# Sample sequences in a gated-linear-attention head: output rows from masked queries in groups of 32 array columns, and state updates from values stacked as rounded part over remainder

## What is computed

```python
q_dec   = q * exp(bcum)              # bcum: running sum of the log decay
k_intra = k * exp(-bcum)
k_state = k * exp(blast - bcum)
att     = where(causal, q_dec @ k_intra.T, 0)
o_intra = att @ v
# per chunk:
o_inter = q_dec @ s                  # s: 128 x 512 state of the head
s       = exp(blast) * s + k_state.T @ v
```

## Time and profile before

| what | value |
|---|---|
| median of 3 runs | 1750.68 us (1748.29 to 1751.83) |
| time of the profiled execution | 1749.48 us |
| its span | 1747.8 us |
| mean granted PE clock | 0.978 |
| PE busy | 1669.8 us, 96% of the span |
| DVE, ACT, POOL busy | 810.9, 481.5, 395.2 us |
| chain that ended last, share on PE | 88% |

### The profile page before, as it was taken

One profiled execution on the slowest core, in us unless ns is written; L12 is line 12 of the kernel. 1 busy time (PEld: TensorE's weight loads), 2 busy tenths in 40 slices (PEclk: granted clock), 3 DMA queues, 4 the chain that ended last, 5 costly groups with the idle time before them and its releaser, 6 DMA issues.

```text
span 1747.8 us, 26517 instructions
## 1 busy us (share of the span) xinstructions
PE 1669.8 (96%) x10399; PEld 1581.4 (90%) x10399; DVE 810.9 (46%) x1188; ACT 481.5 (28%) x1017; POOL 395.2 (23%) x386
## 2 busy tenths in 40 slices
PE   6899999999999999987999999999999999999997
PEld 3799999999999999987998899988999889998796
DVE  4494449443944394456133551234612346213365
ACT  4321111111111111134343313443032531225323
POOL 3221121211221122114132112241212322113210
PEclk8999999999999999988999999999999999999998
DMA  9412212221222122111012111122111121111212
GB/s 351 131 53 73 75 39 65 74 76 39 65 74 76 39 65 74 51 37 37 26 42 79 64 41 49 31 67 79 39 49 37 61 79 39 48 37 55 79 43 102
DMA packets 145621, 115.23 MB, mean 66 GB/s; under 512 B 5885, under 2 KB 128345, under 8 KB 145506
## 3 DMA queue, kind: packets, MB, share of 16 engines
q1 hardware_dynamic: 143680, 112.87, 21.0%
q10 hardware_dynamic: 1834, 0.74, 0.2%
HBM read 99.05 MB, written 15.00 MB: 65 GB/s over the span
## 4 chain that ended last, share of the span: by engine, by line
PE 88%; DVE 8%; ACT 2%; issue 1%; DMA 1%; SPq 0%; ACTq 0%; DVEq 0%
PE psA L506 45%; PE psB L506 29%; PE psB L1798 2%; PE psB L1748 2%; PE psB L1765 2%; PE psX L1730 1%; DVE PQ L1257 1%; PE psX L1787 1%; PE psB L1756 1%; DMA ada<-in_ada_w 1%; DVE y_rows L1499 1%; PE psX L1612 1%; DVE a_hi L582 1%; ACT PQ L1035 1%; DVE PQ L422 0%
## 5 line engine op out<-in xcount | busy, mean ns | idle before, releaser
L313 POOL TENSOR_TENSOR w_lo<-stage,w_hi 128x1024 fp32r<-128x1024 f32 x112 | 279.0, 2491 | 1069.5 <-ACT w_hi L308 1069.5
L506 PE MATMUL psA<-h_hi,w_hi 128*128 128x362 f32 (+1 forms) x1152 | 279.9, 352 | 28.3 <-DVE h_lo L444 15.6
L506 PEld LDWEIGHTS psA<-h_hi,w_hi 128*128 128x128 f32 x1152 | 200.3, 193 | 77.7 <-issue 73.4
L506 PE MATMUL psA<-h_lo,w_hi 128*128 128x362 f32 (+1 forms) x1152 | 255.9, 331 | 0.0
L506 PE MATMUL psA<-h_hi,w_lo 128*128 128x362 f32 (+1 forms) x1152 | 255.7, 330 | 0.0
L308 ACT ACTIVATE w_hi<-stage 128x1024 fp32r<-128x1024 f32 x112 | 120.2, 1073 | 392.2 <-PE psB L506 301.3
L506 PEld LDWEIGHTS psA<-h_hi,w_lo 128*128 128x128 f32 x1152 | 203.1, 191 | 0.0
L506 PEld LDWEIGHTS psA<-h_lo,w_hi 128*128 128x128 f32 x1152 | 203.0, 191 | 0.0
L506 PE MATMUL psB<-h_hi,w_hi 128*128 128x362 f32 (+1 forms) x576 | 129.4, 333 | 1.7 <-ACT kT L1035 1.7
L506 PE MATMUL psB<-h_hi,w_lo 128*128 128x362 f32 (+1 forms) x576 | 126.7, 328 | 0.0
L506 PE MATMUL psB<-h_lo,w_hi 128*128 128x362 f32 (+1 forms) x576 | 126.7, 328 | 0.0
(11 more groups left out here) (297 smaller groups left out, 2307.4 us busy)
## 6 DMA issues: line engine op xcount, KB each, us to landing
stage<-in_gla_w_in SPq DMA_DIRECT2D x40, 512.0 KB, 3.8
stage<-in_pool_w_in SPq DMA_DIRECT2D x32, 512.0 KB, 4.1
ada_stage<-in_ada_w SPq DMA_DIRECT2D x24, 512.0 KB, 3.8
ada<-in_ada_w SPq DMA_DIRECT2D x8, 1024.0 KB, 12.5
stage<-in_pool_w_out SPq DMA_DIRECT2D x16, 512.0 KB, 3.4
v<-in_state_gla SPq DMA_DIRECT2D x32, 256.0 KB, 2.6
out_new_gla_sample<-v SPq DMA_DIRECT2D x32, 256.0 KB, 2.0
stage<-in_gla_w_out SPq DMA_DIRECT2D x16, 512.0 KB, 3.6
```

The lines of the kernel that those rows point to most:

```text
L313: nc.gpsimd.tensor_tensor(w_lo[:, j % 2, :], stage[:, j % 2, :], w_hi[:, j % 2, :].bitcast(f32), ALU.subtract).then_inc(lay.lo_done, 1)
L506: last = nc.tensor.matmul(ps[u][:, t, 0:width], weight(w[:, p, :], k), a[:, k, n0:n0 + width], start=(k == 0 and pas == 0), stop=(k == kt ...
```

## The change

It rearranges the samples' part of the GLA heads:

- Masks, `att_s`, `ksm` and `ksT_s` now have 128 partitions: the 64 sample rows stand twice, in the lower and the upper half. The values of the samples move from `v[0:64, 8, :]` to `v_s`, which holds their rounded part in rows 0 to 63 and the remainder in rows 64 to 127; `v_rows` on DVE makes both. `ksm` is made as rounded part and remainder (two DVE operations in a chain, one buffer of each).
- The state update of a sequence becomes two fp32r matmuls of 128 x 128 by 128 x 512 (`sample_update`).
- The queries are written into `qd_cols`, 8 of every 32 columns, the rest zero. `sample_inter` uses 32 such columns as weights and the old state, 512 wide, as moving operand; sequence b writes PSUM partitions 32(b mod 4) on. It runs for two sequences at a time in the even iterations 2, 4, 6 and 8. Sequences 4 to 7 add onto 0 to 3, in other rows of the same groups.
- After the last of them ACT copies the rows to SBUF (`smp_rows`), and `sample_out` on PE, in iteration 9, first does the intra part with the attention's rounded part and remainder (8 fp32r matmuls), then turns the rows to columns and sorts them with 4 f32 matmuls.
- Transposes of the samples' values, of their keys and their scores are written as two f32 matmuls each, into the lower and the upper 64 partitions.
- The samples' output and the mean squares move from bank `X[1]` to bank `X[0]`; `mean_square` gets a wait for the attention mask of the next chunk.
- POOL's setup has more operations; some small buffers move to memory that is reused later.

```diff
                 def ks_rows(b):
-                    if b >= 2:
-                        dve.wait_ge(smp_upd, g * NB + b - 1)
-                    nc.vector.tensor_scalar(ksm[:, b % 2, :], ksT_s[:], seq_rows[:, b:b + 1], None,
-                                            ALU.mult).then_inc(ksm_ready, 1)
+                    if b >= 1:
+                        dve.wait_ge(smp_upd, g * NB + b)
+                    link(nc.vector.tensor_scalar(ksm[:, 0, :], ksT_s[:], seq_rows[:, b:b + 1], None, ALU.mult))
+                    nc.vector.scalar_tensor_tensor(out=ksm[:, 1, :], in0=ksT_s[:], scalar=seq_rows[:, b:b + 1],
+                                                   in1=ksm[:, 0, :].bitcast(f32), op0=ALU.mult,
+                                                   op1=ALU.subtract).then_inc(ksm_ready, 1)
...
-                    nc.vector.tensor_copy(v[0:NS, NSUP, i * P:(i + 1) * P], ps[1][0:NS, 2, 0:P])\
+                    link(nc.vector.tensor_copy(v_s[:, i * P:(i + 1) * P], ps[1][:, 2, 0:P]))
+                    nc.vector.tensor_tensor(v_s[NS:P, i * P:(i + 1) * P], ps[1][NS:P, 2, 0:P],
+                                            v_s[NS:P, i * P:(i + 1) * P].bitcast(f32), ALU.subtract)\
                         .then_inc(L1.evac[1], 1)
...
-                nc.vector.copy_predicated(att_s[:], causal_s[:], X[0][0:NS, 0:NS]).then_inc(smp_attr, 1)
+                link(nc.vector.copy_predicated(att_s[:], causal_s[:], X[0][:, 0:NS]))
+                link(nc.vector.tensor_copy(att_hi[:], att_s[:]))
+                nc.vector.tensor_tensor(att_lo[:], att_s[:], att_hi[:].bitcast(f32),
+                                        ALU.subtract).then_inc(smp_attr, 1)
...
                 gate_in(2)
+                act.wait_ge(smp_rows_done, g + 1)
+                nc.scalar.activation(smp_rows, X[1], ACT.Copy).then_inc(smp_rows_out, 1)
                 split_slot(L1, GP, act, g, GP.slot["O01"])
                 o_out(NSUP)
...
-                def sample(b):
-                    pe.wait_ge(s0_loaded[b % 4], g * 32 + (b // 4) * 16 + 16)
-                    for e in range(KG):
-                        c = 256 + e * NS + b * TS
-                        last = nc.tensor.matmul(X[1][:, c:c + TS], v[:, b, e * P:(e + 1) * P],
-                                                qd_s[:, b * TS:(b + 1) * TS], start=False,
-                                                stop=(b == NB - 1 and e == KG - 1), skip_group_check=True)
+                def sample_inter(b0):
+                    for b in (b0, b0 + 1):
+                        pe.wait_ge(s0_loaded[b % 4], g * 32 + (b // 4) * 16 + 16)
+                        first = b < 4
+                        rows = slice(CG * (b % 4), CG * (b % 4) + CG)
+                        c = CG * b + (TS if first else 0)
+                        last = nc.tensor.matmul(X[1][rows, :], qd_cols[:, c:c + CG], v[:, b, :], start=first,
+                                                stop=not first)
                     if b == NB - 1:
-                        last.then_inc(smp_o_done, 1)
+                        last.then_inc(smp_rows_done, 1)
+                def sample_update(b):
...
-                    nc.tensor.matmul(ps[1][:, 2, :], ksm[:, b % 2, :], v[0:NS, NSUP, :], start=True,
+                    nc.tensor.matmul(ps[1][:, 2, :], ksm[:, 0, :], v_s[:], start=True, stop=False)
+                    nc.tensor.matmul(ps[1][:, 2, :], ksm[:, 1, :], v_s[:], start=False,
                                      stop=True).then_inc(smp_upd, 1)
+                def sample_out():
+                    pe.wait_ge(smp_attr, g + 1)
+                    for e in range(KG):
+                        for part in (att_hi, att_lo):
+                            nc.tensor.matmul(X[0][:, 256 + e * NS:256 + (e + 1) * NS], v_s[:, e * P:(e + 1) * P],
+                                             part[:], start=(e == 0 and part is att_hi), stop=False,
+                                             skip_group_check=True)
+                    pe.wait_ge(smp_rows_out, g + 1)
+                    for e in range(KG):
+                        last = nc.tensor.matmul(X[0][:, 256 + e * NS:256 + (e + 1) * NS], smp_rows[:, e * P:(e + 1) * P],
+                                                smp_order, start=False, stop=(e == KG - 1), skip_group_check=True)
+                    last.then_inc(smp_o_done, 1)
...
-                sample_intra()
                 fill(FILL_START - 5)
...
                     if 1 <= s <= NSUP:
+                        pe.wait_ge(att_ready, g * NSUP + min(s + 2, NSUP))
                         mean_square(s - 1)
+                    if s in (2, 4, 6, 8):
+                        sample_inter(s - 2)
+                    if s == NSUP + 1:
+                        sample_out()
                     if s >= 2:
-                        sample(s - 2)
+                        sample_update(s - 2)
```

More of the change, by code:

```diff
@@ L172, in trunk @@
         Kp = sb("Kp", [P, 4, SUP], stack=heads)
-        qd_s = sb("qd_s", [P, NS], stack=heads)
         ki_s = sb("ki_s", [P, NS], stack=heads)
         ks_s = sb("ks_s", [P, NS], stack=heads)
-        ksT_s = sb("ksT_s", [NS, P], stack=heads)
-        v = sb("v", [P, NSUP + 1, GW], stack=heads)
+        ksT_s = sb("ksT_s", [P, P], stack=heads)
+        att_lo = sb("att_lo", [P, NS], f32r, stack=heads)
+        v = sb("v", [P, NSUP, GW], stack=heads)
+        v_s = sb("v_s", [P, GW], f32r, stack=heads)
         heads.close()
@@ L185, in trunk @@
         a_lo = sb("a_lo", [P, KG, T], f32r)
+        qd_s = qd_cols[:, TS:TS + NB * CG].rearrange("p (b c) -> p b c", c=CG)[:, :, 0:TS]
+        smp_rows = Kp[:].rearrange("p b t -> p (b t)")
+        smp_order = ident[:].rearrange("p (j c) -> p j c", c=CG)[:, :, 0:2 * TS]\
+            .rearrange("p j (h t) -> p h j t", h=2)
         s1 = PQ[:, 0:WE]
@@ L276, in trunk @@
         S_stored = sem("S_stored")
+        smp_rows_done, smp_rows_out = sem("smp_rows_done"), sem("smp_rows_out")
         smp_o_done, smp_o_evac, smp_ksT = sem("smp_o_done"), sem("smp_o_evac"), sem("smp_ksT")
@@ L804, in _ @@
                                     pattern=[[1, P]], channel_multiplier=-1))
[L806 to L817, removed]
+            link(pool.memset(seq_two[:], 1.0))
@@ new lines, in _ @@
+            link(pool.affine_select(out=seq_two[:], in_=seq_two[:], compare_op=ALU.is_ge, fill=0.0, base=0,
+                                    pattern=[[-NS, 2], [-TS, NB]], channel_multiplier=1))
+            link(pool.affine_select(out=seq_two[:], in_=seq_two[:], compare_op=ALU.is_ge, fill=0.0, base=TS - 1,
+                                    pattern=[[NS, 2], [TS, NB]], channel_multiplier=-1))
+            link(pool.tensor_tensor(seq_rows[:], seq_two[:, 0, :], seq_two[:, 1, :], ALU.add))
@@ new lines, in _ @@
+            causal_two = mod1[:].rearrange("p m c -> p (m c)")[:, 0:2 * NS].rearrange("p (h c) -> p h c", h=2)
+            for h in range(2):
+                cs3 = causal_two[:, h, :].rearrange("p (b t) -> p b t", b=NB)
+                link(pool.memset(cs3, 1.0))
+                link(pool.affine_select(out=cs3, in_=cs3, compare_op=ALU.is_ge, fill=0.0, base=-NS * h,
+                                        pattern=[[-TS, NB], [0, TS]], channel_multiplier=1))
+                link(pool.affine_select(out=cs3, in_=cs3, compare_op=ALU.is_ge, fill=0.0, base=NS * h,
+                                        pattern=[[TS, NB], [1, TS]], channel_multiplier=-1))
@@ L1136, in head @@
                 act.wait_ge(smp_kT, g + 1)
-                nc.scalar.activation(ksT_s[:], ps[1][0:NS, 1, 0:P], ACT.Copy).then_inc(smp_ksT, 1)
+                nc.scalar.activation(ksT_s[:], ps[1][:, 1, 0:P], ACT.Copy).then_inc(smp_ksT, 1)
                 ksT_out(0)
@@ L1690, in v_transpose @@
                     pe.wait_ge(L1.evac[GP.set[src]], evacs(GP, g, src))
[L1691 to L1694, removed]
+                    for s in range(NSUP):
+                        nc.tensor.transpose(ps[GP.set[u]][:, s // 4, (s % 4) * P:(s % 4 + 1) * P],
+                                            vT[i % 2][:, s * P:(s + 1) * P], ident[:])
+                    for half in (slice(0, NS), slice(NS, P)):
+                        last = nc.tensor.matmul(ps[GP.set[u]][half, 2, 0:P], vT[i % 2][:, TP:T], ident[:],
+                                                start=True, stop=True)
                     last.then_inc(L1.unit_done, 1)
@@ L1804, in mean_square @@
                     pe.wait_ge(osum_ready, g * (NSUP + 1) + s + 1)
-                    nc.tensor.matmul(X[1][0:n, s:s + 1], sqo[s % 2][:, 0:n], ones[:, 0:1], start=False,
+                    nc.tensor.matmul(X[0][0:n, P + s:P + s + 1], sqo[s % 2][:, 0:n], ones[:, 0:1], start=False,
                                      stop=True, skip_group_check=True).then_inc(oms_done, 1)
```

46 lines of the change are left out of this document (26 added, 20 removed).

## The result

The changed kernel takes 1722.74 us, the median of 4 runs (1716.72 to 1723.76), against 1750.74 (1748.29 to 1751.83) for the kernel before on the same chip. The ratio is 0.9835, with a 95% interval of 0.981 to 0.986: 28 us faster. The forecast was 1708 and its range 1700 to 1729; the time is that of rival B, 1724.

The account below looks back on a forecast made before the run. PE, busy 96% of the span, was taken to bound the kernel. Removing 89.6 us and adding 47.1 nets 42.5 less than 1749.5, giving 1707.0, or 1708 as median; range 1700 to 1729.

Parts of the forecast that it names:

- rival B: Loop end: POOL comes first and holds DVE's second operation, PE waits about 1.6 us per head, clock falls: 1724; chance 0.3.
- The end of the loop, where it is decided: Loop end: the second half of `ks_rows(7)` on DVE starts 0.03 to 0.1 us before POOL, so isn't held.
- The clock: Loop ends of the four heads: 23.8 us at the lower level; about 10 us entered as removed.
- Rival C: Loop end: no wait, but the clock falls since `sample_out` is weight-load bound; 9 us stay, 1717; chance 0.1.
- update: State update in fp32r on PE: 0.46 us each, 0.1 more for half of them, 16.3 us in all.
- pair of `sample_inter`: Two sequences in two column groups on PE, side by side: 1.2 us a pair, 19.2 us for 16.
- front of a head: Ahead of `sample_scores`: transposes, `v_rows`' additional operation and doubled scores add 0.9 us per head, 3.6 in all.
- What was costed at nothing: Mask operations, second `ks_rows` operation, `mean_square`'s new wait, POOL's setup and earlier state loads: all covered, 0 us.
- rival E: In the loop: a late state load or a DVE wait per iteration takes 10 us: 1718; chance 0.04.
- D: Pairs of `sample_inter` don't overlap, costing 13.8 us: 1722, or 1738 with B; chance 0.08.
- F: Inside the loop: array work in two of four column groups lets the clock fall; about 1780; chance 0.03.
- A: Loop end: the forecast itself, the wait and the low clock go: 1708, own range 1702 to 1714; chance 0.45.

Follow-up runs that it names:

- experiment 1: Changed kernel with ACT splitting O01 after the samples' output and POOL doing its remainder after the sums of squares: 1707.20 us, ratio 0.9749.
- experiment 3: Changed kernel with one added ScalarE operation of 8 columns ahead of the O01 split, written to an unread buffer: 1710.60 us, ratio 0.9779.
- experiment 5: Changed kernel with one sequence of `sample_inter` in each iteration 2 to 9, not two in every second: 1730.29 us, ratio 0.9885.
- experiment 2: Kernel before the change, with the same exchange of order on ACT and POOL as experiment 1: 1741.74 us, ratio 0.9949.
- experiments 8, 9: New outputs alone (old f32 64-row updates), then new updates alone (old 8-column outputs), each with the exchange of experiment 1: 1726.74 us, then 1718.85 us.
- experiment 10: Changed kernel with the exchange of experiment 1 and one filler step moved from behind the samples' scores to ahead of them: 1703.40 us, ratio 0.9731.
- experiment 4: Changed kernel with the update as one f32 product over 128 rows and one DVE operation in `ks_rows`: 1730.69 us, ratio 0.9882.
- 6: Stacked fp32r updates alone, with the old outputs of 8 columns each and no `sample_inter`: 1733.59 us, ratio 0.9904.

## Why the prediction was right in its range and wrong in its number

**The step that failed** is the one under "The end of the loop, where it is decided": that the second half of `ks_rows(7)` would start "0.03 to 0.1 us before POOL". Counted from the start of the last pair, it put DVE's operation at 2.73 us and POOL's at 2.76 to 2.84. Measured from 1180.70, DVE's is at 2.73, to the hundredth; POOL's is at 2.71. POOL's side was 0.05 to 0.13 us late in the sum. ACT's copy starts 1.10 us behind the pair's start, not 1.12. ACT starts its split 0.49 us after the start of its copy, though the copy is 0.60 long (two operations on ACT overlap by 0.1), where 0.5 to 0.56 had been added whole; the earlier trace rows already show such an overlap, as L1126 ends at 1193.95 and L308 starts at 1193.82. And POOL follows 1.12 behind the split, not 1.15. That DVE's side came out to the hundredth is partly luck: 1194.48 and 0.66 give 1195.14 for `ks_rows(7)`, where the sum goes on from 1195.18, and `sample_state(6)` started 0.03 later than forecast (1.75 behind the pair's start, for 1.72), which made up for it. The order is lost by 0.02 us, and rival B came with its price: 7.3 us of wait (B: 6.4). Experiments 1 and 3 show that the order decides: 15.5 and 12.1 us come back (with 5.2 of new wait in the second), where B had put 16. The row of 1.91 us that the prediction sets beside the rule on two SBUF inputs is of an operation with one wide input, L1398; it bears on who comes first, not on the number of inputs.

**The clock** fell with the wait in the changed kernel, as B said: 17.0 us low with it, none at the loop ends without it (experiments 1, 3). It is this wait, of 1.8 us right behind `sample_out`; the waits of up to 1.4 and 1.6 us that experiments 3 and 5 have a few us later leave the clock up. But the prediction took the low clock of the kernel before for a result of the wait there, and experiment 2 refutes that: it stays at 23.8 us with PE busy throughout. The 10 us that I entered as removed do come in experiment 1, which is luck as to the reason: they come with short outputs and 64-row updates taken away, of which either alone left 3.4 to 6.8 us of the 23.8 low (experiments 8, 9), and not because a stall ends. What in that work lets the clock fall stays open. Rival C, the clock falling though nothing waits, is refuted for `sample_out`: the window stays at 1.00 in experiment 1.

**The other terms**, per piece, each against its forecast:

| term | forecast | measured | in all |
|---|---|---|---|
| update | 0.46, +0.1 for half | 0.57 | 18.2 for 16.3 |
| pair of `sample_inter` | 1.2 | 1.05 | 16.8 for 19.2 |
| `sample_out` | 2.0 | 1.7 | 6.8 for 8.0 |
| front of a head | 0.9 | 0.92 | 3.7 for 3.6 |

`sample_out` is read in experiment 1, from 1178.19 to the update's start at 1179.89. The front is 0.45 for the transposes of the last value tile, 0.28 more wait for `ks_s` and 0.19 for the doubled scores and keys; the other three transposes are hidden by waits for ACT that are now gone, as said. The sum of what is added is 45.5, for 47.1. With 89.6 removed this is 44.1 us less, and experiment 1, where PE has no wait for `ksm` and no clock is low at the loop ends, is 42.1 less by its profiled execution (1707.34). Of the 2.0 us between, 1.5 lie ahead of the heads, where the first product of the decay starts at 822.07 in that execution and at 820.56 in the one of the kernel before; 0.5 is not placed. (The eighth updates were entered as 1.1 x 4 = 4.5 where it is 4.4, and the wait as 6.8 where the trace has 6.7.) In experiment 10 the kernel passes the forecast.

**What was costed at nothing** cost nothing: no wait of PE for `v`, `att_ready` or `smp_rows` stands in the answer, and the load of sequence 7 is issued at 1177.21, 3.5 us before the pair that needs it, where the forecast had 3.5 as well (2.6 of landing and 0.9 of cover). So rival E fell. D fell by experiment 5. F fell: of the 1-us windows from 860 to 1700 us only those at the four loop ends have a low clock. Behind the last head, in the last 25 us of the program, every kernel has a low stretch (6.8 us from 1725 us in the kernel before, 3.4 from 1701 in the changed one); these are not explained here.

The chances were sound in one thing: A and B differed in 0.03 us of a sum with 0.05 of error in several terms, so B deserved as much as A. The upper bound of the range had room for B and D, and it held. That B's 1724 is 1.3 us from the measured 1722.7 is in part luck: the prices of the pieces were 1.6 us too high, and the changed kernel's profiled execution was 2.4 us later ahead of the heads (822.91 for 820.56).

## What to carry to other kernels

Where a DVE and a POOL operation are due within some 0.1 us, the order can't be predicted from a sum of durations: give both outcomes the same chance, price both, and then remove the meeting by order (here one exchanged line on two engines, worth 15.5 us, more than half of what the change itself brought). When a piece is shortened, look for long POOL operations that were clear of it before. And don't book a low clock to the wait beside it until a run without the wait has shown the clock come back.

## What was not expected of the hardware

- Two 32-column groups of f32 work cost what one costs: 0.98 us for two sequences or for one (experiment 5), with no extra for the second.
- The lower clock can come without any idle PE: 0.66 over 10 us with PE busy 10.00 us (experiment 2), in a kernel with matmuls of 8 columns, each with its own weight load, and f32 matmuls of 64 rows; with either of them alone 3.4 or 6.8 us were low in place of 23.8 (experiments 8, 9).
- And it can stay up beside idle PE: 1.00 over 10 us with PE busy 8.74 (experiment 3).
- DVE's `TENSOR_SCALAR` with one wide input waits for POOL like the operation with two (2.33 us in experiment 4, 2.40 in 6, for 0.28).
- Two consecutive ACT operations overlap by 0.1 us at their border (copy of 0.60 us, next start after 0.49).
